# Expert quads in another order: the next quad's token gather first, the last quad's combination in two halves

## What is computed

```python
def hier_moe(hn, w_grp, w_exp, w_gate, w_up, w_down):
    ...
    gate = p_g * top_p / jnp.sum(top_p, axis=-1, keepdims=True)
    expert = grp[:, None] * EXPERTS_PER_GROUP + top_i.astype(jnp.int32)
    ...
    def expert_block(args):
        xb, e = args
        hh = jax.nn.silu(xb @ w_gate[e]) * (xb @ w_up[e])
        return hh @ w_down[e]
    ys = lax.map(expert_block, (xs, blk_expert)).reshape(p_slots, d)
    y = jnp.zeros((n + 1, d), ys.dtype).at[slot_tok].add(ys * slot_w[:, None])[:n]
```

## Time and profile before

| | |
|---|---|
| runs | 1864.67, 1864.79, 1867.54 us; median 1864.79 |
| profiled execution | 1863.87 us, span of its instructions 1862.1 us |
| TensorE busy | 1685.6 us (91% of the span), mean granted clock 0.945 |
| VectorE, ScalarE busy | 832.0 us (45%), 653.6 us (35%) |
| DMA | 526.42 MB, mean 283 GB/s |
| expert stages, about | 139 to 595 us (layer 0), 749 to 1204 us (layer 1) |

### The profile page before, as it was taken

The page is one execution under the profiler, slowest core; times in us unless marked ns, Lnnn a source line. Parts: engine busy times, 40 slices in busy tenths (PEclk is TensorE's granted clock), DMA queues, the critical chain, the costliest instruction groups (busy, mean ns, idle before and its releaser), DMA issues.

```text
span 1862.1 us, 31186 instructions
## 1 busy us (share of the span) xinstructions
PE 1685.6 (91%) x12410; PEld 1215.9 (65%) x12410; DVE 832.0 (45%) x1501; ACT 653.6 (35%) x1175; POOL 62.2 (3%) x58
## 2 busy tenths in 40 slices
PE   8999888887889999987878888999999999999997
PEld 8985434243335868533434343599988989998897
DVE  5652122121214664212122121488856656885663
ACT  4431111110113643211111111365547646554763
POOL 1100000000001010000000000100001100000110
PEclk9999888888989999999898898999999999999999
DMA  8669999999999415999999999644532344463232
GB/s 313 237 265 415 421 422 421 421 422 421 422 421 376 136 46 215 414 421 422 421 422 421 421 422 422 282 144 153 203 114 92 113 137 138 157 204 114 91 111 94
DMA packets 89224, 526.42 MB, mean 283 GB/s; under 512 B 10032, under 2 KB 10288, under 8 KB 39728
## 3 DMA queue, kind: packets, MB, share of 16 engines
q1 hardware_dynamic: 89136, 525.19, 71.5%
HBM read 524.10 MB, written 1.05 MB: 282 GB/s over the span
## 4 chain that ended last, share of the span: by engine, by line
PE 58%; DMA 25%; SPq 7%; DVE 6%; ACT 2%; issue 1%; DVEq 0%
DMA arena<-experts 14%; PE banks L504 13%; PE banks L508 11%; PE banks L510 10%; PE banks L509 10%; DMA ring<-experts 10%; SPq L443 7%; PE banks L702 5%; PE banks L684 3%; PE banks L720 3%; DVE hT L1727 1%; DVE arena L1602 1%; DMA ring<-dense 1%; ACT arena L1443 1%; PE banks L565 1%
## 5 line engine op out<-in xcount | busy, mean ns | idle before, releaser
L508 PE MATMUL banks<-arena_parts,ring_parts 128*128 128x256 f32 (+1 forms) x1444 | 418.5, 290 | 8.8 <-ACT arena L1157 6.1
L510 PE MATMUL banks<-arena_parts,ring_parts 128*128 128x256 f32 (+1 forms) x1444 | 410.3, 284 | 0.0
L509 PE MATMUL banks<-arena_parts,ring_parts 128*128 128x256 f32 (+1 forms) x1444 | 409.6, 284 | 0.0
L504 PEld LDWEIGHTS banks<-arena 128*128 128x128 f32 (+1 forms) x2512 | 302.4, 191 | 58.1 <-issue 45.8
L504 PE MATMUL banks<-arena 128*128 128x128 f32 (+3 forms) x2512 | 335.8, 288 | 1.9 <-ACT arena L1157 1.3
L702 PE MATMUL banks<-ring,arena 128*32 128x512 f32 x1536 | 233.0, 710 | 105.4 <-DMA ring<-experts 105.4
L1157 ACT ACTIVATE arena<-banks 128x256 f32<-128x256 f32 (+6 forms) x370 | 159.2, 456 | 405.9 <-PE banks L504 163.1
L1582 DVE TENSOR_TENSOR ring_parts<-ring,ring_parts 128x1024 fp32r<-128x1024 f32 x204 | 244.9, 1233 | 98.1 <-ACT ring_parts L1157 86.3
L508 PEld LDWEIGHTS banks<-arena_parts,ring_parts 128*128 128x128 f32 x1444 | 273.9, 190 | 17.0 <-issue 7.1
L1157 ACT ACTIVATE ring_parts<-ring 128x1024 fp32r<-128x1024 f32 x208 | 215.3, 1055 | 186.1 <-DMA ring<-dense 185.1
L509 PEld LDWEIGHTS banks<-arena_parts,ring_parts 128*128 128x128 f32 x1444 | 274.1, 190 | 0.3
(11 more groups left out here) (223 smaller groups left out, 1584.6 us busy)
## 6 DMA issues: line engine op xcount, KB each, us to landing
ring<-experts SPq DMA_DIRECT2D x192, 1024.0 KB, 26.5
arena<-experts SPq DMA_DIRECT2D x160, 1024.0 KB, 22.2
ring<-dense SPq DMA_DIRECT2D x224, 512.0 KB, 4.9
at<-experts SPq DMA_DIRECT2D x16, 1024.0 KB, 24.1
x<-experts SPq DMA_DIRECT2D x16, 1024.0 KB, 22.5
consts<-consts_in SPq DMA_DIRECT2D x1, 1414.0 KB, 12.5
vecs<-vecs_in SPq DMA_DIRECT2D x1, 1125.5 KB, 14.6
hT<-h_in SPq DMA_DIRECT2D x2, 544.0 KB, 4.6
```

The costliest lines, as they stand in the source:

```text
L504: return pe.matmul(o, lhsT, rhs, start=(k == 0), stop=(k == n - 1))
L508: pe.matmul(o, lhsT[0], rhs[0], start=(k == 0), stop=False)
L509: pe.matmul(o, lhsT[0], rhs[1], start=False, stop=False)
L510: return pe.matmul(o, lhsT[1], rhs[0], start=False, stop=(k == n - 1))
```

## The change

In a quad, TensorE now gathers the next quad's tokens first, ahead of this quad's gate and up products; for that it waits for both copies of this quad's tokens at once. The combination of the last quad is cut into two halves of four columns, one ahead of the transposes of the gated rows and one behind them. VectorE follows: four additions, then the copy of the transposed rows, then the other four.

```diff
-                def combine(i):
-
-                    pe.wait_ge(s["ya_ready"], i + 1)
-                    pe.wait_ge(s["yd_ready"], i + 1)
-                    pe.wait_ge(s["sw_ready"], i + 1)
-                    for c in range(DC):
+                def combine(i, chunks=range(DC)):
+
+                    if chunks[0] == 0:
+                        pe.wait_ge(s["ya_ready"], i + 1)
+                        pe.wait_ge(s["yd_ready"], i + 1)
+                        pe.wait_ge(s["sw_ready"], i + 1)
+                    for c in chunks:
...
+                    pe.wait_ge(s["xs_ready"], i * 2 + 2)
+                    prep(i + 2)
                     for k in range(8):
-                        if k % 4 == 0:
-                            pe.wait_ge(s["xs_ready"], i * 2 + (k // 4 + 1))
                         w = weights(k)
...
                         m.then_inc(s["used"], 1)
-                    prep(i + 2)
+                    combine(i, range(4))
                     pe.wait_ge(s["h_ready"], i + 1)
                     for k in range(2):
                         m = pe.transpose(psum[:, 3, k * P:k * P + P], mo_h[:, k * P:k * P + P], C("ident"))
                     m.then_inc(s["ht_done"], 1)
-                    combine(i)
+                    combine(i, range(4, DC))
...
                     v.tensor_tensor(mo_h, mo_silu, psum[:, 3, 256:512], ALU.mult).then_inc(s["h_ready"], 1)
+                    v.wait_ge(s["add_done"], i * DC + 1)
+                    for c in range(4):
+                        add(i, c)
                     v.wait_ge(s["ht_done"], i + 1)
                     v.tensor_copy(wide(mo_ht), psum[:, 3, 0:256]).then_inc(s["ht_ready"], 1)
-                    v.wait_ge(s["add_done"], i * DC + 1)
-                    for c in range(DC):
+                    for c in range(4, DC):
                         add(i, c)
```

## The result

The changed kernel takes 1875.12 us (median of five runs, 1872.77 to 1875.64) against 1865.73 us of the kernel before on the same chip: a ratio of 1.0044, 95% interval 1.0032 to 1.0055, so slower by 6.0 to 10.3 us. The profiled execution took 1874.65 us with a span of 1872.8 us, 10.7 us more than the 1862.1 of before.

A forecast was written before the change was run, and what follows sets the result against it. DMA was taken to bound the expert stages' body, an empty queue the head, TensorE the tail. +14.9 head, 0 body, -4.7 tail and -1.3 clock gave +8.9 us: 1873.3 us, range 1868.3 to 1878.

The forecast's parts named there:

- What bounds the stages: Expert stages: DMA sets the pace in the body, TensorE has 8.6 us spare per quad; only head and tail count.
- The head, +14.9: Loop start, both layers: prep and its selection wait delay q0's gate products 7.67 and 7.24 us, paid in full.
- The body, 0: Middle quads: a 2.69 us selection wait per quad, covered by the spare 8.6 us, costs nothing.
- The tail, -4.7 without the clock: Behind q14's unit 6: 5.66 us of prep out, 2.69 wait and 0.6 split in; 2.4 gained per layer.
- the split, +0.6 per tail: Split combination in the tail's two quads: late first additions and the copy between additions cost 0.3 us per quad.
- The clock, -1.3: q14's last two gate units, both layers: half clock may come too late to hurt; half of 2.6 us taken.
- the whole 2.6 us of my bound: Both tails: most that full clock in q14's last two gate units could gain, 1.74 + 0.86 us.
- rival D: Tail: wait and later gaps bring half clock into its unbroken work, 2.5 us more per layer; 1879.6 us, chance 0.07.
- Rival A: Head: three units still queued hide the later start, leaving the tail's gain; -6 us, 1858, chance 0.05.
- Rival C: q1: queue runs dry a second time despite 5.6 us in hand; 1879 with 3 us per layer, chance 0.05.
- B: No difference: 5 us or more of the head's 14.9 absent; 1863 to 1868.5 us, chance 0.08.
- My row for "2 us of idle time don't cost the clock": q0's 2 us wait: no clock cost, since TensorE idled 1.2 of 2 us at 130 to 132 at 1.00.

The follow-up runs named there:

- head_only: Kernel before, with prep ahead of the gate products in q0 of each layer alone; 1883.76 against 1866.69 us, ratio 1.0094.
- body_only: Kernel before, with prep first in q2 to q13 only, no split; 1866.21 against 1866.1 us, ratio 0.9995.
- body_double: Kernel before, with prep first in q2 to q13 only and each of these preps made twice; 1874.41 us, ratio 1.0045.
- delay_4: Kernel before, order unchanged, with four idle products ahead of each layer's loop; 1871.68 against 1865.3 us, ratio 1.0032.
- q0_kept: Changed kernel, with q0 of each layer back in the old order; 1862.21 us against 1866.69 of the kernel before, ratio 0.9976.
- early_select: Changed kernel, with q0 and q1 in old order and VectorE's selections ahead of the down products' copy; 1854.59 us against 1865.3 before, ratio 0.9936.
- split_only: Kernel before, with the combination split around the transposes and prep in its old place; 1863.28 against 1866.69 us, ratio 0.9984.
- gather_only: Changed kernel without the split, whole combination behind the transposes, VectorE's old order; 1881.16 us against 1866.69 of the kernel before, ratio 1.0074.

## Why the prediction was right, point by point

**What bounds the stages.** Right. The expert stages are a train of 163 units behind the loop's first issue, and at the head this issue is the moment that counts. head_only (the head alone, +17.5) and body_only (24 quads, nothing) show both halves of the statement, and body_double shows where it ends.

**The head, +14.9.** Right in layer 0: gate products foreseen at 146.66, found at 146.65; SP's issue foreseen at 148.0, found at 148.00. Layer 1: 7.24 foreseen, 8.26 found, since prep(1) ran at half clock there and the selection for the second prep waits for its end. Sum found 15.9, foreseen 14.9. head_only has it at 17.5 (14.6 to 20.7), and delay_4 found 6.0 (3.9 to 8.2) for 6.9 us of delay.

**The body, 0.** Right, by body_only and by the same 409.4 us in both profiles.

**The tail, -4.7 without the clock.** The terms: prep out, 5.66 and 5.46; the wait, 2.69 foreseen, 2.60 found (570.65 less 568.05, where the down products of 567.19 end by their usual 0.86 us) and about 2.5 in layer 1; the split, +0.6 per tail foreseen, -0.1 found. This last term was mis-sized, to the wrong side: from the end of the gate products to L714 it is 4.91 us (559.26 to 564.17), where the transposes and the whole combination took 4.97 before. The late `mo_h` is there (VectorE's first addition starts at 560.15, 0.89 us behind the first combination product, in place of 0.73), but the 0.22 us of the transposes are hidden in return. I had added what the split delays and had not asked what it covers. Without the clock the tails gained 6.1 us (3.14 + 3.78 less the 0.8 below), not 4.7.

**The clock, -1.3.** About right in sum, and by luck. q14's two last gate units were at full clock in both tails (559.26 less 557.40, 1.86 us, against 3.57; 1.85 against 2.69 in layer 1), the whole 2.6 us of my bound. The way there was another than mine in layer 0: I had the gate products catch up with the arrivals at about the fourth unit, but q14's prep ran at half clock (543.38 to 550.56), and so they started late and ran without a wait up to unit 6. In other kernels that gather first those two units were at half clock in one tail or in both (3.57 us in layer 1 of q0_kept, 3.36 in layer 0 of early_select). At the same time rival D came true in part: q15's prep in layer 0 took 7.19 us in place of 5.46, at half clock, behind the wait of 2.42 us. The stretches of this place:

```profile
570.00:571.00 1.00, 0.35 (x3) 0.35 (x4) 0.56 (x1) 0.00 (x0) 0.00 (x0) 1.00 0.99 410
571.00:572.00 1.00, 1.00 (x8) 1.00 (x7) 0.00 (x0) 0.00 (x0) 0.00 (x0) 0.53 1.00 418
572.00:573.00 1.00, 1.00 (x6) 1.00 (x6) 0.00 (x0) 0.00 (x0) 0.00 (x0) 0.50 1.03 426
...
575.00:576.00 1.00, 1.00 (x12) 1.00 (x11) 0.00 (x0) 0.00 (x0) 0.00 (x0) 1.00 1.01 418
```

The clock falls to half when the engine is already at work again, and costs 1.7 us there. Net in the tails: -2.55 + 1.73 = -0.8. With prep(1) of layer 1 (7.22 us) the clock's sum over the kernel is close to nothing.

**Sum.** Foreseen +8.9 for the profiled execution, found 10.8; the medians differ by 9.4, and by the ratio it is 6.0 to 10.3. That the sum fits so well is luck in part: the head cost 1.0 us more than foreseen (layer 1's slow prep(1)), the tails gained 0.9 more (15.9 less 6.9 is 9.0), and the other 1.8 of the 10.8 are in stages that the change doesn't touch, which I had put at nothing. These stages differ by 3 us between the profiles of kernels that are alike in them: from the last combination of layer 0 to prep(1) of layer 1 it is 153.02 us in the kernel before, 153.69 in the changed one and 155.96 in q0_kept, and the second block takes 661.54 us in split_only and 664.55 in q0_kept. So a microsecond or two of one profile's span says nothing about the change; only the rows of the stage itself do. Rival A (a reserve in the queue) fell with delay_4. Rival C (dry a second time) is not seen in the changed kernel: its arrivals keep step (409.4 us in both), although q1's gate products start at 172.18, 1.2 us later than foreseen. B did not happen, and D did in small.

**My row for "2 us of idle time don't cost the clock" was no evidence.** I inferred it from 1.2 us of idle time at 130 to 132 us. In the changed kernel q0's second prep did run at full clock (5.55 us behind 1.99 us of waiting), but in gather_only, in the same place and behind the same wait, it did not:

```profile
141.03 7.25 PE L504 MATMUL banks<-arena 128*128 128x128 f32 x48 [1.98 <-DVE arena L1738]
148.22 5.36 PE L715 MATMUL banks<-ring,arena 128*32 128x512 f32 x48
```

That one cost the head 1.6 us more. In these traces such a wait has two prices, nothing or 1.6 to 1.7 us, and the head's term carried only the first. The Trainium skill (TensorE: Matmul & The Clock Gate, What's actually happening) calls the monitor's window free-running, not tied to the program, which fits a wait that costs the clock in one execution and not in another.

## What to carry to other kernels

Where a stage is bound by its transfers, cost a reordering at the first use that frees a buffer and at the last arrival, not by the count of quads: work moved ahead of the first use is paid in full if the queue is just running dry there, the same work in the body is free up to the slack per turn, and behind the last arrival it is paid again. An order that is good for the tail can be kept for the tail and given up for the first turn: here +8 us became -4 by writing q0 out, and -12 once VectorE no longer did the selection behind a wait for TensorE. Dropping an unread prep as well gave -14, which is not clear of noise against -12. A look at the DMA's GB/s in one-microsecond stretches around the first issue tells which case it is.

## What the runs showed of the hardware that I had not expected

The granted clock fell to 0.50 within the first microsecond of dense work *after* an idle time of 2.42 us (571 us above), and a prep (48 products in the trace) then took 7.25 us in place of 5.62; behind waits of 1.98 us (gather_only) and 1.99 us (the changed kernel) in the same place it fell in one profile and not in the other. The length of the wait doesn't decide it: behind 2.60 us in q1 of q0_kept (163.28 us) the prep took 5.60 us, at full clock, and behind 2.34 us in q15 of layer 1 it took 5.63 us in the changed kernel and 7.26 in gather_only. In layer 1 of the changed kernel it fell at 748 us, after an idle time of 1.45 us and 1.4 us of products. What sets the moment of the fall is not shown here.
